# Attention outputs turned by two plain transposes whose halves VectorE adds, in place of two full-precision products with stacked identities

## The reference, cut to what matters

```
def one_block(args):
    qn, qr, qb = args
    s = jnp.einsum('bqhd,bkhd->bhqk', qn, k_nope) + jnp.einsum('bqhr,bkr->bhqk', qr, k_rope)
    s = s.astype(jnp.float32) * scale
    mask = key_chunk[None, :] <= q_chunk[:, None]
    p = jax.nn.softmax(jnp.where(mask, s, -jnp.inf), axis=-1).astype(v.dtype)
    return jnp.einsum('bhqk,bkhd->bqhd', p, v)
```

## Time and profile before

| | |
|---|---|
| median of 3 runs | 2447.23 us (2442.8 to 2447.33) |
| profiled execution, first to last instruction (its span) | 2443.0 us |
| PE busy | 2241.9 us, 92% |
| PEld busy | 1894.6 us, 78% |
| DVE busy | 1624.7 us, 67% |
| ACT busy | 1225.4 us, 50% |
| phase B in the trace | 630 to 1240 us of the span |

### The profile page before, as it was taken

The page is one execution under the profiler, slowest core; times in us unless marked ns, Lnnn a source line. Parts: engine busy times, 40 slices in busy tenths (PEclk is TensorE's granted clock), DMA queues, the critical chain, the costliest instruction groups (busy, mean ns, idle before and its releaser), DMA issues. The chain is left out here.

```text
span 2443.0 us, 42737 instructions
## 1 busy us (share of the span) xinstructions
PE 2241.9 (92%) x13522; PEld 1894.6 (78%) x13523; DVE 1624.7 (67%) x2948; ACT 1225.4 (50%) x2007; POOL 359.3 (15%) x255
## 2 busy tenths in 40 slices
PE   7999999998899999989979995999999999999970
PEld 7899999897677777777868885777777788888760
DVE  5444454456777778778866786686886765656646
ACT  5333333324666676767742220665666555554536
POOL 0000000000100000000001111124242322323226
PEclk9999999998999999999999996999999999999995
DMA  4122211251000000000144334798999978968837
GB/s 178 61 76 81 76 60 60 91 168 61 6 6 9 14 7 17 5 7 11 50 152 155 144 120 155 261 358 300 365 318 355 333 223 276 314 215 263 308 90 281
DMA packets 157243, 368.34 MB, mean 151 GB/s; under 512 B 25793, under 2 KB 37825, under 8 KB 155201
## 3 DMA queue, kind: packets, MB, share of 16 engines
q1 hardware_dynamic: 142592, 318.88, 35.8%
q0 software_dynamic: 13104, 47.72, 8.0%
q10 hardware_dynamic: 1440, 0.37, 0.1%
HBM read 295.11 MB, written 72.35 MB: 150 GB/s over the span
## 5 line engine op out<-in xcount | busy, mean ns | idle before, releaser
L2041 PE MATMUL eH<-w_hi,at_tok 128*128 128x512 f32 x720 | 288.2, 400 | 10.4 <-DVE at_tok L2159 10.4
L2042 PE MATMUL eH<-w_hi,at_tok 128*128 128x512 f32 x720 | 285.6, 397 | 0.0
L2092 ACT CAST w_hi<-w_raw 128x4096 fp32r (+1 forms) x64 | 232.7, 3635 | 103.6 <-DMA w_raw<-in_w 69.4
L2101 DVE TENSOR_TENSOR w_raw<-w_raw,w_hi 128x4096 f32 (+1 forms) x64 | 282.6, 4417 | 0.2 <-issue 0.2
L1105 ACT CAST prT_hi<-pT 128x512 fp32r<-128x512 f32 (+1 forms) x288 | 162.3, 564 | 148.8 <-PE pT L1009 147.5
L2101 DVE TENSOR_TENSOR w_raw<-w_raw,at_row 128x4096 f32 x32 | 141.7, 4428 | 127.1 <-ACT at_row L2092 126.9
L1225 DVE TENSOR_TENSOR prT_lo<-pT,prT_hi 128x512 fp32r<-128x512 f32 (+1 forms) x288 | 188.2, 656 | 56.6 <-ACT prT_hi L1105 54.5
L1143 POOL TENSOR_TENSOR qT_lo<-q_raw,qT_hi 128x512 fp32r<-128x512 f32 x32 | 40.9, 1278 | 1148.6 <-ACT qT_hi L1087 1148.6
L1216 DVE TENSOR_REDUCE mx<-pS 128x1 f32<-128x512 f32 (+2 forms) x320 | 191.2, 608 | 13.5 <-PE pS L999 6.8
L2046 PE MATMUL eH<-w_raw,at_tok 128*128 x720 | 184.1, 397 | 7.6 <-DVE w_raw L2101 7.4
L2046 PEld LDWEIGHTS eH<-w_raw,at_tok 128*128 128x128 f32 x720 | 133.8, 187 | 45.9 <-issue 14.6
(11 more groups left out here) (371 smaller groups left out, 5685.4 us busy)
## 6 DMA issues: line engine op xcount, KB each, us to landing
w_raw<-in_w SPq DMA_DIRECT2D x96, 2048.0 KB, 13.6
xt<-in_x SPq DMA_DIRECT2D x9, 1024.0 KB, 8.0
xs<-in_x SPq DMA_DIRECT2D x8, 1024.0 KB, 5.0
scratch_h<-hp SPq DMA_DIRECT2D x16, 512.0 KB, 2.7
scratch_z<-hp SPq DMA_DIRECT2D x16, 512.0 KB, 3.6
fz<-scratch_z SPq DMA_DIRECT2D x16, 512.0 KB, 7.9
out<-fz SPq DMA_DIRECT2D x16, 512.0 KB, 2.6
scratch_xT<-xT_hi SPq DMA_DIRECT2D x7, 1024.0 KB, 4.0
```

What stands on the lines that cost most here:

```text
L2041: pe.matmul(H[:], xh[:, k, :], w.hi[:, k, :], start=(k == 0), stop=False)
L2042: pe.matmul(H[:], xl[:, k, :], w.hi[:, k, :], start=False, stop=False)
L2092: nc.scalar.copy(w.hi[:], w.words(o).bitcast(F32)).then_inc(w.hi_ready, 1)
L2101: v.tensor_tensor(w.words(o), w.words(o).bitcast(F32), w.hi[:].bitcast(F32), ALU.subtract).then_inc(w.lo_ready, 1)
```

## The change: what it does

The two full-precision products of `fold` become two transposes (`pe.transpose`) of the 128x128 tiles of `oT` against the identity. Each writes 128 columns of `pO` in place of 64: queries down, and across first the 64 channels of the high part, then the 64 of the low part. VectorE's `divide` gets a first instruction that adds the two halves, a `tensor_reduce` over a rearranged view of 256 columns whose innermost axis is the pair of halves, into `a_out`. After a wait on a semaphore of its own it multiplies `a_out` in place with the reciprocals. The constant `stack` goes: its array, its buffer and its DMA.

```diff
@@ shape_constants
-    c["stack"] = (s[:, None] % VD == s[None, :VD]).astype(np.float32)
@@ phase_a, block.scalar
-                    (t["gq"][:], d["q_norm_g"]), (t["gkv"][:], d["kv_norm_g"]), (t["fold"][:], d["fold"]), (t["stack"][:], d["stack"]),
+                    (t["gq"][:], d["q_norm_g"]), (t["gkv"][:], d["kv_norm_g"]), (t["fold"][:], d["fold"]),
-                act.wait_ge(const_loaded, 128)
+                act.wait_ge(const_loaded, 112)
@@ phase_a, block.vector
-                v.wait_ge(const_loaded, 128)
+                v.wait_ge(const_loaded, 112)
@@ phase_b
-        o_copied = sem("o_copied"); o_folded = sem("o_folded"); cleared = sem("cleared"); rs_ready = sem("rs_ready"); rin_ready = sem("rin_ready")
+        o_copied = sem("o_copied"); o_folded = sem("o_folded"); o_summed = sem("o_summed"); cleared = sem("cleared"); rs_ready = sem("rs_ready"); rin_ready = sem("rin_ready")
@@ phase_b, fold(n)
                     for i in range(2):
-                        ins = pe.matmul(O[n % 2][:, 2 * P + i * VD:2 * P + (i + 1) * VD], oT[:, n % 2, i * P:(i + 1) * P], t["stack"][:],
-                                        start=True, stop=True)
+                        ins = pe.transpose(O[n % 2][:, (2 + i) * P:(3 + i) * P], oT[:, n % 2, i * P:(i + 1) * P], t["ident"][:])
@@ phase_b, divide(n)
-                    v.tensor_tensor(a[:, n % 4], O[n % 2][:, 2 * P:2 * P + 2 * VD].rearrange("p (i c) -> p i c", i=2),
-                                    rin[:, both].unsqueeze(2).broadcast_to([P, 2, VD]), ALU.mult).then_inc(a_ready, 1)
+                    v.tensor_reduce(a[:, n % 4], O[n % 2][:, 2 * P:4 * P].rearrange("p (i x c) -> p i c x", i=2, x=2), AX, ALU.add).then_inc(o_summed, 1)
+                    v.wait_ge(o_summed, n + 1)
+                    v.tensor_tensor(a[:, n % 4], a[:, n % 4], rin[:, both].unsqueeze(2).broadcast_to([P, 2, VD]), ALU.mult).then_inc(a_ready, 1)
@@ build
-        keep(ctx, "stack", [P, VD])
```

## The result

The changed kernel takes 2449.9 us (median of 17 runs, 2444.7 to 2452.7) against 2445.2 for the kernel before (17 runs, 2442.8 to 2448.0). The ratio is 1.0016, with a 95% interval from 1.0009 to 1.0023: 3.9 us slower, between 2.2 and 5.6 (the ratio weighs all runs; the two medians alone are 4.8 apart). The forecast was 2.1 us slower.

What follows compares the result with a forecast made beforehand. Phase B was taken as bound by PE in some steps and by VectorE's chain of maxima and rests in others. Losses 5.8 less savings 3.7 gave +2.1 us; on the median 2447.2 that is 2449, range 2445 to 2457.

Steps and rivals of the forecast that it cites:

- the likeliest case: Whole kernel: mostly no change, within 0.2% or 4.9 us; chance of same 0.62.
- The prices: VectorE's divide: reduce 0.425, wait 0.03, multiply holding 0.21, together 0.665 against 0.20, so 0.465 added to each.
- Rival 3: VectorE's divide: the reduce of pairs costs 0.69 or more, giving 2455; chance 0.09.
- Where VectorE's 0.465 shows: Phase B: the added 0.465 is hidden where VectorE has cover and lost elsewhere; losses sum to 5.8 us.
- The divides of 12 and 44: Phase B, step 12 of each sixteen: VectorE idles behind the divide, so the added time is covered at no cost.
- Step 58: Phase B: the next link of the maxima's chain follows the divide closely, so 0.31 is lost.
- What a fold gives back: PE in phase B: slot 0.39 becomes 0.22, 0.17 saved, surviving in 22 folds: 3.7 us.
- The end: End of the stage: weigh waits for one divide and another is the last work, two in series: 0.93 lost.
- rival 4: Phase B's clock: if its falls doubled, some +3 us, 2452; chance 0.03.
- rival 1: Phase B: PE sets the time in all steps, VectorE's cover is larger; 10.9 less 0.93, 2437; chance 0.10.
- rival 2: Phase B: VectorE sets the time, cover at the second wait is missing; 11.5 us sticks out, 2459; chance 0.13.
- Rival 2's own sign: Waits view of phase B: PE's waits on VectorE's rest would grow well beyond 41.

Runs made afterwards that it cites:

- e2: Kernel before with only divide changed: a reduce over pairs, a wait, then the multiply in SBUF; ratio 1.0029 to the kernel before, 7.1 us slower.
- e8: Kernel before, unchanged, run again for a second profile: span 2441.9 us, no falls of the clock in the stretch.
- e5: Changed kernel with divide one slot later on VectorE for steps 6 and 7 of each sixteen alone; ratio 1.0002 to the kernel before.
- e1: Changed kernel with the old single multiply on the high halves only, low halves left out; ratio 0.9983 to the kernel before, 4.1 us faster.
- e3: Changed kernel with the constant stack still declared, loaded and waited for, but not used; ratio 1.0015 to the kernel before.
- e7: Changed kernel with low halves multiplied on ScalarE and two scalar_tensor_tensor adding on VectorE; ratio 1.0039 to the kernel before, 9.5 us slower.

## Why the prediction was right, and where it was not

The time, the direction and the size of change were inside what was forecast: 2449.9 against 2449, slower by 3.9 against 2.1, within 0.2% of the old time as the likeliest case had it. That the times agree to 1 us is in part luck. The forecast stood on a median of three runs, 2447.2, and the median of 17 is 2445.2; from there its 2.1 would have given 2447.3. And of the 6.3 us between the mean spans of the profiles (2448.5 of three against 2442.1 of four), the mechanism that it priced holds 2.3.

- **The prices** on VectorE were right. Reduce 0.416 against 0.425, multiply 0.292 as taken, the whole divide 0.66 against 0.665. Rival 3, a reduce of pairs at 0.69, is out. The multiply from SBUF took 0.292 and the old one from the bank 0.282, on the same 128 columns. The Trainium skill, VectorE: DVE Perf Modes, "The TRN2 errata", puts the fixed part lower for SBUF than for PSUM; this case's traces don't agree.
- **Where VectorE's 0.465 shows** was right in thirteen places of the table to 0.04. In the stretch the losses of e2 without falls are 4.5 us, forecast 4.9, and two places that falls cover in that profile would add 0.9. Two terms were wrong. The divides of 12 and 44 were called covered; they cost 0.45 where no fall lies over them. Their cover in the first trace was there because falls at 768 and 1086 us had slowed PE: the instruction behind the divide of 12 had 1.34 of idle time ahead of it, and in e8, where no fall was, it started 0.02 after the divide's end.
```profile
773.77 0.70 DVE L1179 TENSOR_TENSOR q_raw<-pS,trig 64x512 f32<-64x512 f32 x1 [1.34 <-PE pS L977]
```
  The same divide in step 28, with no fall near, had shown cover of 0.11 only, and that difference within a pattern was the hint. Step 58, priced 0.31, cost nothing.
- **What a fold gives back** was counted too low. The new slot was right (0.21 against 0.22), but the old one is the prediction's 0.39, or 0.40, in 27 folds, all ahead of a turn, and not in 50. In the 25 folds ahead of a score product it is 0.44 to 0.46 where no fall lies over it, and 0.24 is saved. 22 folds at 0.17 were 3.7 us; the PE half alone has 5.2, the changed kernel's steps 3.8. Which folds survive was right in part: that of step 5 came through (0.16 to 0.18), though a wait on VectorE's chain was thought to take it, and the one of 12 did not. Those of 14 to 16, forecast as 15 and 0 of each sixteen, offset the late divide of 14.
- **Net in the stretch, falls aside**: 584.4 against 582.6, +1.8, forecast +1.1 (4.87 of loss less 3.7). The 584.4 is put together from the four profiles of the change, each step taken where no fall lies near it, two of them from e5. So far the account is shown; that the terms wrong on both sides nearly cancel is luck.
- **The end**: forecast 0.93 of loss, which is what e2 shows (11.30 against 10.37). In the changed kernel the last divide came only 0.48 later against the step's start, for PE's two folds there save time too (e1: 0.44 less), a term that the forecast put into e1's account and not into its own. The next stage came another 1.2 later in three profiles of four, in step with the load of instructions beside the last stores; e3 has neither. Why the instructions are loaded just there in some of these programs and not in others wasn't tried.
- **The clock**: rival 4 put a chance of 0.03 on more falls and a price of 3 us on them. In the profiles they came: three in place of 1.0 on average, 4.0 us of falls against 1.45, 2.6 more. This is the largest term that the sum lacked. (The rival's price was low by its own rows: 1% of 610 us of clock is 12 us at half rate, not 6.) That the profiles differ, 3, 3, 3, 3 against 3, 0, 1, 0, is measured; the cause stays open. The Trainium skill, TensorE: Matmul & The Clock Gate, Part 4, says that transposes don't count as activity for the clock gate. The falls of the profiles don't follow that rule here: e1 and e7 have the transposes and one fall each, e2 has the old products and the long divides and two. But in the timed runs e1's clock too is 0.0010 under that of the kernel before, 1.4 falls' worth, while e7's is equal to it, so a part played by the transposes is neither shown nor excluded. It may be where in time the short steps fall and not how long PE idles in them.

The sum by the profiles is 1.8 + 0.5 + 1.1 + 2.6 = 6.0, near the 6.3 between the mean spans (0.3 is there before step 4 already, and the stages behind attention add nothing) and above the 3.9 of the timed runs. With its lowest run at 2444.7, the changed kernel too may have executions with fewer falls than these four show.

Against the rivals: rival 1 fails by e1 (4.1, not 10.9), rival 2 by the places in the table and by e5, where moving eight divides takes 2.6 us off the steps without less work on VectorE. Rival 2's own sign, PE's waits on the rest well beyond 41, didn't come: they are 49 or 50.

## What to carry to other kernels

Work moved from the busiest engine to the second busiest is paid not by the sum but at the places where the second engine's next instruction has no idle time ahead of it, and where the first engine's saving meets a wait on the second. Walk one period of the schedule, note for each place the idle time and the slack of the consumer, and price what is saved at each place by the instruction that follows it there. Here most single places came out to 0.04 us, and the net to 0.7. Take cover only from a stretch at full clock, and look whether the same place in another period has it too. If a loss sits in few places, move those instructions by one slot rather than all of them.

## What was not expected of the hardware

- Step times of an in-order, hand-pipelined stage repeat between executions of one program to 0.05 us each. All scatter of the stage in the kernel before came as single stretches at 1.2 GHz, 1.4 to 1.65 us each: the stretch was 582.5 to 587.2 for the same program.
- The reduce over pairs with a stride of 64 elements, read from the bank, took 0.416, less than the maxima over as many contiguous columns (0.425); 128 results cost nothing extra.
- scalar_tensor_tensor over 64 columns took 0.280, as long as a tensor_tensor over 128 (0.282).
- A load of instructions of 0.02 MB that stood among the last stores before a barrier went with 0.9 to 1.25 us more before the next stage, in six profiles of six; the eight without it had 0.1 at most.
